# Attention scores: the two components of a head interleaved on TensorE, the causal masks issued ahead of them

## Chip, cores and metric

One core of a Trainium2 chip (trn2) runs the whole program in one launch. The metric is device microseconds (us) of one execution, the median of several; lower is better.

## What is computed

One inference step of a two-layer decoder: a prompt of 1024 tokens and eight sample tokens go through RMSNorm, a joint input projection, a pooling mixer beside differential attention (4 heads), an output projection and a convolution-gated FFN. The change lies in the prompt's attention:

```
def diff_core(q, k, v, q_pos, k_pos, lam):
    s = jnp.einsum('bqhcd,bkhcd->bhcqk', q, k).astype(F32) * (HEAD_DIM ** -0.5)
    mask = k_pos[None, :] <= q_pos[:, None]
    s = jnp.where(mask, s, -jnp.inf)
    p = jax.nn.softmax(s, axis=-1)
    a = p[:, :, 0] - lam * p[:, :, 1]
    return jnp.einsum('bhqk,bkhe->bqhe', a.astype(v.dtype), v)
```

Each head has two components `c` of 64 dimensions, with a softmax each; their difference weighs the values. HEAD_DIM is 64, VDIM is 128, and queries are taken in 8 blocks of 128.

## The kernel before

All 1032 tokens stay in SBUF with the features on the partitions. A head runs in two parts. First come its projections (`up_unit`, L921), pooling and key reshaping, and the pooling half of the output projection (`down_part`, L950). Then comes the attention of its 8 query blocks, in the order `ORDER = [7, 0, 6, 1, 5, 2, 4, 3]`: step s handles block i = ORDER[s], whose scores are (i+1)*128 wide. Two layers of four heads make eight such attentions.

`qT` and `kT` hold component 0 of the head on partitions 0 to 63 and component 1 on partitions 64 to 127. PSUM has two groups of three banks (`group0`, `group1`, guarded by the semaphores `g_free` and `g_full`), one bank for transposes (`t_bank`), one for outputs (`o_bank`); the third bank of each group holds the transposes of the attention weights (`p_bank`) and the sample outputs (`s_bank`). Component 0 of a step takes one group, component 1 the other.

One step s crosses the engines like this:

- TensorE, `scores(s)`: for each component, after a wait for its group, the score matmuls against the keys before the block (L1085, at most 512 columns each), the block on the diagonal (L1088), and the mask, a bf16 product that adds minus 2^100 above the diagonal (L1090), with the semaphore increment that says that the group is full.
- VectorE, `maxima(s)`: for each component the row maximum (L1460) and from it the bias (L1461).
- ScalarE, `exps(s)`: for each component the exponential with its row sum (L764), which frees the group.
- VectorE, `combine(s)`: joins the two components (L1470, L1471, L1474).
- TensorE, `weigh(s)`: transposes of the weights (L1112), for steps 4 to 7 the sample values (`values`, L1097), then the product with the values (L1132), once ScalarE has copied the transposes (L792, L796). `turn_out(s - 1)` (L1141) follows.

TensorE's queue is written out by hand: `scores(0)`, the value transposes `turn("v", ...)` (L1056), and then for each s: `scores(s + 1)`, `weigh(s)`, `turn_out(s - 1)`, with the sample softmax after step 1 (L1166, L1168) and its weights after step 3 (L1157). ScalarE's queue for step s is `mix(s - 2)` (L780), `squares(s - 1)` (L774), the copies of the transposes, `exps(s + 1)`; VectorE's is `mix(s - 2)` (L1489), `combine(s)`, `normalise(s - 1)` (L1483), `maxima(s + 1)`. Ahead of `exps(0)` ScalarE copies the transposed values (L751), issues the store of them (L754) and splits a weight tile (L630).

Of the kernel before, what the change touches and what calls it, by code (L numbers as in the profile page):

```python
# [17 lines left out]
P = 128  # L18
# [7 lines left out]
N_HEADS, HEAD_DIM = 4, 64  # L26
# [134 lines left out]
def hybrid_decoder_kernel(nc, x_prompt, x_sample, cache_k, cache_v, state_pool, state_conv, page_table, norm1_g, w_in,  # L161
# [4 lines left out]
    with ExitStack() as ctx:  # L166
        def sb(name, shape, dt=F32):
            return ctx.enter_context(nc.sbuf_tensor(name, shape, dt))

        def sem(name):  # L170
            return ctx.enter_context(nc.semaphore(name))
# [10 lines left out]
        mask = sb("mask", [P, 2, P], BF16)  # L182
# [5 lines left out]
        qT = sb("qT", [P, T])  # L188
        kT = sb("kT", [P, T])
# [20 lines left out]
        bank = ctx.enter_context(nc.psum_tensor("bank", [P, 8, 512], F32))  # L210
# [16 lines left out]
        g_full, g_free = [sem("group0_full"), sem("group1_full")], [sem("group0_free"), sem("group1_free")]  # L227
# [76 lines left out]
        def x_buf(t):  # L304

            if t < 3:
                return scratch[:, 1024 * t:1024 * t + 1024]
            if t < 7:
                return page[:, t - 3, :, :].rearrange("p t d -> p (t d)")
            return (qT, kT)[t - 7][:, 0:1024]  # L310
# [5 lines left out]
        def grp(p):  # L316
            return bank[:, 3 * p:3 * p + 3, :]
# [40 lines left out]
        def use(half, j):  # L358
            return j % 2, half + j // 2

        def use_head(l, h, name):
            return use(G_SETUP // 2 + l * (G_LAYER // 2) + h * (G_HEAD // 2), HG[name])
# [538 lines left out]
        def _(pe):  # L901
            def wait_free(u):
                pe.wait_ge(g_free[u[0]], u[1] + 1)
# [69 lines left out]
            for t in range(QT_N + 1):  # L973
                u = use(0, t)
                wait_free(u)
                pe.wait_ge(x_in[t], 16)
                rows = P if t < QT_N else 8
                g = bank[:, 3 * u[0]:3 * u[0] + 2, :].rearrange("p a b -> p (a b)")
                for k in range(KC):
                    ins = pe.transpose(g[:, k * P:k * P + rows], x_buf(t)[0:rows, k * P:(k + 1) * P],  # L980
                                       ident[0:rows, 0:rows])
                ins.then_inc(g_full[u[0]], 1)
            u = use(0, QT_N + 1)
            wait_free(u)
            pe.wait_ge(params_in, 16 * len(PAR) * DEPTH)
            for l in range(DEPTH):
                ins = pe.transpose(bank[:, 3 * u[0], l * P:l * P + PAR_W], k_tok[0:PAR_W, l, :],
                                   ident[0:PAR_W, 0:PAR_W])
# [27 lines left out]
            with pe.Fori(0, DEPTH) as l:  # L1016
                norm(l * 2, l * T_LAYER)
                with pe.Fori(0, N_HEADS) as h:
                    it = l * N_HEADS + h
                    n0 = l * U_LAYER + h * U_HEAD  # L1020
                    ug = lambda name: use_head(l, h, name)
# [14 lines left out]
                    for n in range(2):  # L1036
                        u = ug(("qb", n))
# [4 lines left out]
                    u = ug(("y",))  # L1042
# [3 lines left out]
                    for t in range(NT):  # L1046
                        ins = pe.matmul(grp(u[0])[:, t, 0:TW], pw[:, :], pool_dd[:, t * TW:(t + 1) * TW],
                                        start=True, stop=True)
# [25 lines left out]

                    def scores(s):
                        i = ORDER[s]
                        width = (i + 1) * P
                        for c in range(2):
                            u = ug(("s", s, c))
                            wait_free(u)  # L1080
                            rows = slice(c * HEAD_DIM, (c + 1) * HEAD_DIM)

                            for n, at in enumerate(range(0, i * P, 512)):
                                w = min(512, i * P - at)
                                pe.matmul(bank[:, 3 * u[0] + n, 0:w], qT[rows, i * P:(i + 1) * P],  # L1085
                                          kT[rows, at:at + w], start=True, stop=True)
                            last = bank[:, 3 * u[0] + i // 4, (i % 4) * P:(i % 4 + 1) * P]
                            pe.matmul(last, qT[rows, i * P:(i + 1) * P], kT[rows, i * P:(i + 1) * P],  # L1088
                                      start=True, stop=False)
                            ins = pe.matmul(last, mask[:, 0, :], mask[:, 1, :], start=False, stop=True)  # L1090
                            ins.then_inc(g_full[u[0]], 1)

                    def values(b):

# [41 lines left out]
                    def turn_out(s):  # L1136
# [5 lines left out]
                                  stop=True).then_inc(t_full, 1)  # L1142

                    scores(0)
                    turn("v", 0, v_T)
                    turn("v", 1, v_T)
                    for s in range(QT_N):
                        if s + 1 < QT_N:
                            scores(s + 1)
                        weigh(s)  # L1150
                        if s >= 1:
                            turn_out(s - 1)
                        if s == WEIGHTS_STEP:

                            pe.wait_ge(soft_sel, it + 1)
                            for j in range(N_PAGES):
                                ins = pe.matmul(s_bank[:, j * 8:j * 8 + 8], soft[:, j * P:(j + 1) * P], sel8,  # L1157
                                                start=True, stop=True)
                            ins.then_inc(weights_full, 1)
                        if s == SOFTMAX_STEP:  # L1160

                            u = ug(("soft",))
                            wait_free(u)
                            pe.wait_ge(k_red, (it + 1) * DEC_BATCH)
                            for j in range(N_PAGES):
                                pe.transpose(bank[0:16, 3 * u[0] + j // 4, (j % 4) * P:(j % 4 + 1) * P],  # L1166
                                             s_score[:, :, :, j], ident)
                            pe.matmul(bank[0:16, 3 * u[0] + 2, 0:1], comp8, ones[:, 0:1], start=True, stop=True  # L1168
                                      ).then_inc(g_full[u[0]], 1)
# [48 lines left out]
            for t in range(QT_N + 1):  # L1218
                rows = P if t < QT_N else 8
                ins = pe.matmul(t_bank[0:rows, t:t + 1], rot[:, t * P:t * P + rows], ones[:, 0:1], start=True,  # L1220
                                stop=True)
            ins.then_inc(t_full, 1)
            pe.wait_ge(y_done, 2 * DEPTH * NT * KC + KC)
            for t in range(QT_N + 1):
                u = use(G_SETUP // 2 + DEPTH * (G_LAYER // 2), t)
                wait_free(u)
                rows = P if t < QT_N else 8
                g = bank[:, 3 * u[0]:3 * u[0] + 2, :].rearrange("p a b -> p (a b)")
                for k in range(KC):
                    ins = pe.transpose(g[0:rows, k * P:(k + 1) * P], resid[:, k, t * P:t * P + rows], ident)  # L1230
# [391 lines left out]
```

## Time and profile before

| | |
|---|---|
| median of 3 runs | 3089.33 us (3088.89 to 3091.76) |
| span of the profiled execution | 3088.1 us |
| TensorE busy | 2837.5 us, 92% of the span |
| VectorE, ScalarE, GpSimd busy | 1545.4, 785.2, 932.2 us |
| mean granted TensorE clock | 0.936 |

The span runs from the first to the last instruction of the profiled execution. The profile gives no other time of that execution: what lies outside its span is seen only against the runs, whose median is 1.2 us above it. A matmul record is modelled at its end, so records of one stream overlap; the start of one record to the start of the next tells the rate. An fp32 matmul shows as two records here (two passes), each with its own weight load (PEld). A weight load starts when the stream ahead of it does, so its start also marks that of the stream before.

### The profile page before, as it was taken

Reading aid. Unit: us, or ns where it says so; the run is one execution under the profiler, and the core shown is the slowest. Engines: PE = TensorE matmul, PEld = TensorE weight load, DVE = VectorE, ACT = ScalarE, POOL = GpSimd, SP = SyncE. Lnnn points to the kernel's source line nnn. Section 1 sums busy time; section 2 is a strip of 40 time slices with the busy share of each in tenths; the row PEclk is TensorE's granted clock in tenths of the full one; section 3 lists DMA queues with packets and bytes.
Section 4 is the critical chain, followed back from the end, with each engine's and each line's share of the span. In section 5 each row is a group of like instructions: output and inputs, shape, how many; then the busy total and the mean of one; then the engine's idle time right before and its main releaser. Section 6 shows DMA issues by size and latency. Waiting matters only on the chain.

```text
span 3088.1 us, 45465 instructions
## 1 busy us (share of the span) xinstructions
PE 2837.5 (92%) x16776; PEld 2587.2 (84%) x16776; DVE 1545.4 (50%) x1931; ACT 785.2 (25%) x1516; POOL 932.2 (30%) x768
## 2 busy tenths in 40 slices
PE   5889898988999999999988989888999999999996
PEld 4768686867999999999876867777789999999996
DVE  5746464555443444444575463647454444443435
ACT  3221313134222222222233131222332222222222
POOL 4624333244212212221254252525242121212220
PEclk7999898988999999999988998889889999999998
DMA  3422222121111111111113222321111111111111
GB/s 119 125 69 66 89 69 82 49 82 38 46 41 41 55 48 41 41 41 47 52 51 98 68 91 68 99 62 58 52 49 41 41 41 51 52 41 41 41 41 55
DMA packets 70800, 184.00 MB, mean 60 GB/s; under 512 B 8014, under 2 KB 28936, under 8 KB 70552
## 3 DMA queue, kind: packets, MB, share of 16 engines
q1 hardware_dynamic: 33352, 105.95, 10.1%
q0 software_dynamic: 18496, 67.58, 7.0%
q10 hardware_dynamic: 18848, 8.96, 1.0%
q8 instruction: 81, 1.33, 0.2%
q14 instruction: 23, 0.19, 0.0%
HBM read 169.27 MB, written 13.64 MB: 59 GB/s over the span
## 4 chain that ended last, share of the span: by engine, by line
PE 51%; issue 29%; POOL 10%; DVE 6%; ACT 2%; SPq 1%; POOLq 0%; ACTq 0%; DMA 0%; DVEq 0%
PE bank L921 22%; PE bank L950 9%; PE bank L1097 4%; POOL w_lo L498 4%; PE bank L1085 4%; PE bank L967 3%; PE bank L939 3%; PE bank L1132 3%; POOL act_lo L525 2%; PE bank L1112 1%; POOL page L562 1%; DVE rot L1412 1%; ACT scratch L764 1%; DVE scratch L1474 1%; POOL page L584 1%
## 5 line engine op out<-in xcount | busy, mean ns | idle before, releaser
L498 POOL TENSOR_TENSOR w_lo<-w_raw,w_hi 128x1024 fp32r<-128x1024 f32 x180 | 441.5, 2454 | 1474.2 <-ACT w_hi L630 1474.0
L1375 DVE TENSOR_TENSOR resid<-bank,resid 128x1032 f32<-128x1032 f32 x400 | 489.9, 1231 | 431.0 <-PE bank L950 431.0
L921 PE MATMUL bank<-act_hi,w_hi 128*128 128x344 f32 x2640 | 570.3, 324 | 0.0
L921 PE MATMUL bank<-act_hi,w_lo 128*128 128x344 f32 x2640 | 560.5, 320 | 0.0
L921 PE MATMUL bank<-act_lo,w_hi 128*128 128x344 f32 x2640 | 556.5, 319 | 0.0
L921 PEld LDWEIGHTS bank<-act_hi,w_hi 128*128 128x128 f32 x2640 | 439.6, 188 | 9.3 <-issue 0.4
L921 PEld LDWEIGHTS bank<-act_hi,w_lo 128*128 128x128 f32 x2640 | 446.3, 189 | 0.0
L921 PEld LDWEIGHTS bank<-act_lo,w_hi 128*128 128x128 f32 x2640 | 439.6, 188 | 0.0
L950 PE MATMUL bank<-mix_hi,w_hi 128*128 128x344 f32 x1200 | 291.5, 352 | 36.3 <-DVE resid L1375 36.3
L950 PE MATMUL bank<-mix_lo,w_hi 128*128 128x344 f32 x1200 | 259.3, 325 | 0.0
L950 PE MATMUL bank<-mix_hi,w_lo 128*128 128x344 f32 x1200 | 258.1, 324 | 0.0
L950 PEld LDWEIGHTS bank<-mix_hi,w_hi 128*128 128x128 f32 x1200 | 188.0, 192 | 73.6 <-DVE resid L1375 42.8
L1543 DVE TENSOR_TENSOR rot<-bank,rot 128x1032 f32<-128x1032 f32 x44 | 54.2, 1233 | 332.0 <-PE bank L921 332.0
L630 ACT ACTIVATE w_hi<-w_raw 128x1024 fp32r<-128x1024 f32 x180 | 188.5, 1048 | 106.5 <-PE bank L967 83.5
L950 PEld LDWEIGHTS bank<-mix_lo,w_hi 128*128 128x128 f32 x1200 | 205.5, 191 | 0.0
L950 PEld LDWEIGHTS bank<-mix_hi,w_lo 128*128 128x128 f32 x1200 | 204.9, 191 | 0.0
L843 ACT ACTIVATE rot<-scratch 128x1024 f32<-128x1024 f32 x44 | 46.7, 1062 | 518.2 <-DVE scratch L1537 518.2
L562 POOL TENSOR_TENSOR page<-page,bq 128x1024 f32<-128x1024 f32 x64 | 156.6, 2465 | 68.0 <-ACT bq L719 67.6
L1085 PE MATMUL bank<-kT,qT 64*128 64x512 f32 (+3 forms) x320 | 133.1, 521 | 7.5 <-DVE resid L1375 4.7
L1097 PE MATMUL bank<-page,rot 128*8 128x128 f32 x1024 | 130.7, 291 | 0.0
L1369 DVE TENSOR_TENSOR resid<-bank,resid 128x688 f32<-128x688 f32 x120 | 104.9, 875 | 40.3 <-PE bank L967 36.1
L1097 PEld LDWEIGHTS bank<-page,rot 128*8 128x8 f32 x1024 | 95.6, 96 | 32.6 <-issue 6.7
(235 smaller groups left out, 3661.9 us busy)
## 6 DMA issues: line engine op xcount, KB each, us to landing
w_raw<-in_w_up SPq DMA_DIRECT2D x88, 512.0 KB, 3.5
w_raw<-in_w_down SPq DMA_DIRECT2D x44, 512.0 KB, 3.4
w_raw<-in_w_in SPq DMA_DIRECT2D x32, 512.0 KB, 3.4
w_raw<-in_w_out SPq DMA_DIRECT2D x16, 512.0 KB, 3.4
out<-v_tok ACTq DMA_DIRECT2D x16, 512.0 KB, 3.4
page<-in_x_prompt SPq DMA_DIRECT2D x4, 512.0 KB, 9.6
out<-page SPq DMA_DIRECT2D x4, 512.0 KB
out<-rows_out ACTq DMA_DIRECT2D x104, 4.0 KB
```

The source lines that it names most:

```text
L498: pool.tensor_tensor(w_lo[:, slot, :], w_raw[:, slot, :], w_hi[:, slot, :].bitcast(F32), ALU.subtract).then_inc(w_lo_done, 1)
L562: pool.tensor_tensor(kp, kp, q_row, ALU.mult).then_inc(k_mul, 1)
L630: act.activation(w_hi[:, off % SLOTS, :], w_raw[:, off % SLOTS, :], ACT.Copy).then_inc(w_hi_done, 1)
L921: ins = pe.matmul(g[:, t, 0:TW], w[:, slot, k * P:(k + 1) * P], x[:, k, t * TW:(t + 1) * TW], start=(k == 0 and n_ == 0), stop=(k == KC - ...
L939: ins = pe.matmul(g[:, T_ORDER[i], 0:TW], w[:, slot, k * P:(k + 1) * P], x[:, k, tile_of(i)], start=(k == 0 and n_ == 0), stop=(k == KC - ...
L950: ins = pe.matmul(g[:, t, 0:TW], w[:, slot, m * P:(m + 1) * P], x[:, t * TW:(t + 1) * TW], start=(n_ == 0), stop=(n_ == 2))
L967: ins = pe.matmul(grp(u[0])[:, a, 0:TW], w[:, slot, m * P:(m + 1) * P], x[:, tile_of(i)], start=(n_ == 0), stop=(n_ == 2))
L1085: pe.matmul(bank[:, 3 * u[0] + n, 0:w], qT[rows, i * P:(i + 1) * P], kT[rows, at:at + w], start=True, stop=True)
L1097: ins = pe.matmul(s_bank[0:8, 0:P], spread[:, t, b, :], page[:, b % 4, t, :], start=(b == 0 and t == 0), stop=False)
L1132: ins = pe.matmul(o_bank[:, 0:P], a_T[:, r, n * P:(n + 1) * P], v_tok[:, b, :], start=(b == 0), stop=(b == i))
L1369: dve.tensor_tensor(rows, grp3(u[0])[:, 0:2, :], rows, ALU.add).then_inc(g_free[u[0]], 1)
L1375: dve.tensor_tensor(tiles(resid[:, m, :]), grp3(u[0]), tiles(resid[:, m, :]), ALU.add).then_inc(g_free[u[0]], 1)
```

## The change

Only `scores` changes. For both components it first waits for the group and issues the mask, now the product that starts the accumulation in the bank that holds the diagonal. Then the score matmuls follow, component 0 and component 1 in turn for each piece of the keys, then the two diagonal blocks, each with its group's increment. The products and their shapes are the same.

```
                     def scores(s):
                         i = ORDER[s]
-                        width = (i + 1) * P
-                        for c in range(2):
-                            u = ug(("s", s, c))
+                        both = (ug(("s", s, 0)), ug(("s", s, 1)))
+                        halves = (slice(0, HEAD_DIM), slice(HEAD_DIM, 2 * HEAD_DIM))
+                        for u in both:
                             wait_free(u)
-                            rows = slice(c * HEAD_DIM, (c + 1) * HEAD_DIM)
-
-                            for n, at in enumerate(range(0, i * P, 512)):
-                                w = min(512, i * P - at)
+                            pe.matmul(bank[:, 3 * u[0] + i // 4, (i % 4) * P:(i % 4 + 1) * P], mask[:, 0, :],
+                                      mask[:, 1, :], start=True, stop=False)
+
+                        for n, at in enumerate(range(0, i * P, 512)):
+                            w = min(512, i * P - at)
+                            own = n < i // 4
+                            for u, rows in zip(both, halves):
                                 pe.matmul(bank[:, 3 * u[0] + n, 0:w], qT[rows, i * P:(i + 1) * P],
-                                          kT[rows, at:at + w], start=True, stop=True)
-                            last = bank[:, 3 * u[0] + i // 4, (i % 4) * P:(i % 4 + 1) * P]
-                            pe.matmul(last, qT[rows, i * P:(i + 1) * P], kT[rows, i * P:(i + 1) * P],
-                                      start=True, stop=False)
-                            ins = pe.matmul(last, mask[:, 0, :], mask[:, 1, :], start=False, stop=True)
-                            ins.then_inc(g_full[u[0]], 1)
+                                          kT[rows, at:at + w], start=own, stop=own)
+                        for u, rows in zip(both, halves):
+                            pe.matmul(bank[:, 3 * u[0] + i // 4, (i % 4) * P:(i % 4 + 1) * P],
+                                      qT[rows, i * P:(i + 1) * P], kT[rows, i * P:(i + 1) * P],
+                                      start=False, stop=True).then_inc(g_full[u[0]], 1)
```

TensorE's order at step 0 (block 7), from the first score matmul to the value transposes. `bank` is PSUM; the last figures are the shape of the output. Before:

```order
L1085 MATMUL bank<-kT,qT 128x512 [waits group1_free]
L1085 MATMUL bank<-kT,qT 128x384
L1088 MATMUL bank<-kT,qT 128x128
L1090 MATMUL bank<-mask 128x128
L903 REGISTER_ALU
L1085 MATMUL bank<-kT,qT 128x512 [waits group0_free]
L1085 MATMUL bank<-kT,qT 128x384
L1088 MATMUL bank<-kT,qT 128x128
L1090 MATMUL bank<-mask 128x128
L906 REGISTER_ALU
L1056 MATMUL bank<-con,rot 128x128 [waits tbank_free]
```

and now:

```order
L1081 MATMUL bank<-mask 128x128 [waits group1_free]
L903 REGISTER_ALU
L1081 MATMUL bank<-mask 128x128 [waits group0_free]
L1088 MATMUL bank<-kT,qT 128x512 x2
L1088 MATMUL bank<-kT,qT 128x384 x2
L1091 MATMUL bank<-kT,qT 128x128 x2
L906 REGISTER_ALU
L1056 MATMUL bank<-con,rot 128x128 [waits tbank_free]
```

Both masks and both waits moved to the front, and each x2 is one matmul of either component.

TensorE's order at step 2 (block 6), which stands behind `weigh(0)` and ahead of the transposes of step 1. Before:

```order
L1085 MATMUL bank<-kT,qT 128x512 [waits group1_free]
L1085 MATMUL bank<-kT,qT 128x256
L1088 MATMUL bank<-kT,qT 128x128
L1090 MATMUL bank<-mask 128x128
L903 REGISTER_ALU
L1085 MATMUL bank<-kT,qT 128x512 [waits group0_free]
L1085 MATMUL bank<-kT,qT 128x256
L1088 MATMUL bank<-kT,qT 128x128
L1090 MATMUL bank<-mask 128x128
L1104 REGISTER_ALU
L1112 MATMUL bank<-con,scratch 128x128 [waits pbank_free,att_weights]
```

and now:

```order
L1081 MATMUL bank<-mask 128x128 [waits group1_free]
L903 REGISTER_ALU
L1081 MATMUL bank<-mask 128x128 [waits group0_free]
L1088 MATMUL bank<-kT,qT 128x512 x2
L1088 MATMUL bank<-kT,qT 128x256 x2
L1091 MATMUL bank<-kT,qT 128x128 x2
L1106 REGISTER_ALU
L1114 MATMUL bank<-con,scratch 128x128 [waits pbank_free,att_weights]
```

The first component's last product, which lets VectorE begin, stood fourth of eight and now stands seventh of eight.

## Rows read from the trace of the kernel before

**Rows 1.** The page: the chain that ended last, by engine and line.
```profile
PE bank L921 22%; PE bank L950 9%; PE bank L1097 4%; POOL w_lo L498 4%; PE bank L1085 4%; PE bank L967 3%; PE bank L939 3%; PE bank L1132 3%; POOL act_lo L525 2%; PE bank L1112 1%; POOL page L562 1%; DVE rot L1412 1%; ACT scratch L764 1%; DVE scratch L1474 1%; POOL page L584 1%
```

**Rows 2.** First head's attention: us, busy of PE, PEld, DVE, ACT, POOL, then PEclk.
```profile
136.70:213.60 76.90, 64.10 (x379) 47.12 (x379) 34.88 (x92) 27.56 (x77) 23.01 (x41) 0.89 0.24 76
```

**Rows 3.** Waits of TensorE, whole span: waiter <- awaited: us, times, longest.
```profile
PE bank L1112 <- DVE scratch L1474: 32.6, 26, 2.0
```

**Rows 4.** Timeline of the weight loads, step 0, component 0: start us, us.
```profile
137.32 0.19 PEld L1085 LDWEIGHTS bank<-kT,qT 64*128 64x128 f32 x1 [0.24 <-issue]
137.75 0.19 PEld L1085 LDWEIGHTS bank<-kT,qT 64*128 64x128 f32 x1 [0.24 <-issue]
138.07 0.51 PEld L1088 LDWEIGHTS bank<-kT,qT 64*128 64x128 f32 x2
138.70 0.10 PEld L1090 LDWEIGHTS bank<-mask 128*128 128x128 bf16 x1
138.86 0.29 PEld L1085 LDWEIGHTS bank<-kT,qT 64*128 64x128 f32 x2
```

**Rows 5.** Timeline, step 0, from its scores to its exponentials.
```profile
136.78 1.77 PE L1085 MATMUL bank<-kT,qT 64*128 64x512 f32 x4 [0.57 <-DVE resid L1375]
...
140.85 0.61 PE L1056 MATMUL bank<-con,rot 128*128 128x128 f32 x4
...
143.53 0.40 ACTq L754 DMA_DIRECT2D out<-v_tok  x1
144.05 1.06 ACT L630 ACTIVATE w_hi<-w_raw 128x1024 fp32r<-128x1024 f32 x1 [0.56 <-ACT v_tok L751]
145.01 1.10 ACT L764 ACTIVATE scratch<-bank,stat 128x1024 f32<-128x1024 f32 x1
```

**Rows 6.** Timeline, scores of step 2 and what follows them.
```profile
153.54 1.55 PE L1085 MATMUL bank<-kT,qT 64*128 64x512 f32 x4
...
155.51 1.09 DVE L1460 TENSOR_REDUCE stat<-bank 128x1 f32<-128x896 f32 x1
...
157.11 0.23 PE L1090 MATMUL bank<-mask 128*128 128x128 bf16 x1
157.18 0.28 PE L1112 MATMUL bank<-con,scratch 128*128 128x128 f32 x1
...
157.67 1.00 ACT L764 ACTIVATE scratch<-bank,stat 128x896 f32<-128x896 f32 x1
...
160.10 1.01 ACT L805 ACTIVATE bq<-bank 16x1024 f32<-16x1024 f32 x1 [0.31 <-PE bank L1168]
```

**Rows 7.** Timeline, step 4: the first maximum, and TensorE's next wait.
```profile
169.15 0.95 DVE L1460 TENSOR_REDUCE stat<-bank 128x1 f32<-128x768 f32 x1
...
172.30 3.26 PE L1157 MATMUL bank<-small,bq 16*128 16x8 f32 x16 [0.46 <-DVE small L1515]
```

**Rows 8.** Timeline, scores of step 5, in head 0 and in head 1.
```profile
175.49 1.22 PE L1085 MATMUL bank<-kT,qT 64*128 64x256 f32 x2
...
176.91 1.02 DVE L1474 SCALAR_TENSOR_TENSOR scratch<-scratch,stat 128x768 f32<-128x768 f32 x1
...
178.95 1.49 PE L1112 MATMUL bank<-con,scratch 128*128 128x128 f32 x6
...
341.61 0.70 PE L1085 MATMUL bank<-kT,qT 64*128 64x256 f32 x2
...
344.10 1.11 PE L1112 MATMUL bank<-con,scratch 128*128 128x128 f32 x4 [0.28 <-DVE scratch L1474]
```

**Rows 9.** Timeline, steps 6 and 7: the weights joined, then transposed.
```profile
188.36 0.62 DVE L1474 SCALAR_TENSOR_TENSOR scratch<-scratch,stat 128x384 f32<-128x384 f32 x1 [0.23 <-DVE stat L1471]
...
189.72 0.50 PE L1112 MATMUL bank<-con,scratch 128*128 128x128 f32 x3
...
196.04 0.88 DVE L1474 SCALAR_TENSOR_TENSOR scratch<-scratch,stat 128x640 f32<-128x640 f32 x1
...
197.18 0.72 PE L1112 MATMUL bank<-con,scratch 128*128 128x128 f32 x5
```

## The prediction

> **What bounds the kernel now.** I read the page's chain first. Most of it is the projections, which the change doesn't touch; the score matmuls L1085 hold 4% [rows 1], some 120 us. They lie in the eight attentions, so I took the first head's apart. It lasts 76.90 us, with TensorE busy for 64.10, at a mean granted clock of 0.89 [rows 2]. The reader is to see that TensorE isn't saturated there: it waits for others, others for it, and a shorter score block is worth only what the next wait leaves of it. Over all eight heads the transposes L1112 waited 26 times for `combine` (L1474), 32.6 us in all [rows 3]: in every head at steps 0, 2 and 7, which makes 24, and twice at step 4. (The scores of step s stand ahead of the transposes of step s - 1.) In the other steps TensorE came to the transposes last, its scores just ahead of them. There the change can pay.
>
> **The price of a score block.** The passes of 512 columns follow each other by 137.75 - 137.32 = 0.43 us, those of 384 by 138.07 - 137.75 = 0.32 [rows 4]. By columns, 256 take 0.21 and 128 take 0.107. Each fp32 product is two passes. From the start of a block (136.78) to the first even pass are 0.43 + 0.11, so the first weight load costs 0.11 [rows 4, 5]. The diagonal's passes begin at 138.39 and last 0.21; the mask's load starts at 138.70, so going from 64 rows of the array to 128 costs 0.10. From the mask back to 64 rows takes 0.16 [rows 4], against 0.07 from a mask to another product of 128 rows [rows 6]. With S for the passes of one product of each width (block 7: 0.43 + 0.32 + 0.107), a block takes 4S + 0.65 now: 3.42 + 0.65 = 4.07, which is what stands between 136.78 and 140.85 [rows 5].
>
> Afterwards both masks come first (0.07, then 0.16), one weight load is bare (0.11), and one change back remains (0.10): 0.44 of fixed cost in place of 0.65. **This 0.21 is sure**, if the halves cost nothing to alternate.
>
> The rest hangs on what the trace of before never shows: a product on rows 0 to 63 directly followed by one on rows 64 to 127. Bound it from both sides. At worst each change of half costs what a change between 64 and 128 rows does, 0.10 to 0.16 [rows 4]. At best the two halves stream side by side. I take the best, since a score product fills 64 rows and leaves the others empty, and the two components share neither array rows, nor input partitions, nor banks. Starts stay in program order, and a pass must wait for the one before it on its own half. So the second component starts one pass late, and a block takes w + 2S + 0.44, w being its first pass. The gain of a block is then 2S - w + 0.21: 1.49 for block 7 (1.71 - 0.43 + 0.21), 1.28 for block 6, 1.06 for 5, 0.85 for 4, 0.74 for 3, 0.64 for 2, and 0.21 for 1 and 0. A block of 128 columns gains less still, one weight load per 0.11 being all that shows.
>
> The Trainium skill ("TensorE: Matmul & The Clock Gate", Part 3) says that matmuls whose operands lie on different row groups run at the same time, and gives 3.07 times for four groups of 32 rows. No row of before can confirm it, and the figure is for another split. "TensorEngine Tiling (Array Packing)", Key Properties, says that changing the tiling mode drains the engine while changing the tile doesn't; the 0.10 and 0.16 agree with the first half. By a drain at every change of tile the result would be the third case below.
>
> **What each step's scores keep of it.**
> - Step 0 (block 7). The value transposes at 140.85 follow the scores; ScalarE copies them, issues the store at 143.53, splits a weight tile at 144.05 and begins the exponentials at 145.01 [rows 5]. All of it hangs in a row behind TensorE, and the maxima are done long before. 1.49 is kept.
> - Step 1 (block 0) runs while ScalarE and `combine(0)` work, and the same at step 3: 0. Here the change adds a wait, since component 0 now waits for component 1's group as well. Behind it stand only the transposes, which wait for `combine` anyway.
> - Step 2 (block 6). Scores start at 153.54, transposes at 157.18, and at 157.67 come the exponentials [rows 6]. Now the block ends at 153.54 + 0.44 + 1.93 = 155.91. Component 0 is full some 0.2 earlier, at about 155.75, later than before: its maximum started at 155.51. With 1.09 for the maximum and 0.2 for the bias its exponentials start at 157.1, not 157.67. 0.5 is kept, and passes on to the sample softmax, whose copy waits for TensorE (160.10).
> - Step 4 (block 5). VectorE begins the maximum at 169.15, when it is free, and everything up to L1157 (172.30) hangs on VectorE [rows 7]. 0, though TensorE gains 1.06.
> - Step 5 (block 2). In head 0 the passes run at 1.2 GHz (1.22 us for the two where head 1 takes 0.70). The transposes start at 178.95, while L1474 is done at 177.93, so 0.95 of some 1.1 is kept. In head 1, at 2.4 GHz, they wait for VectorE anyway [rows 8]. Two of the 26 waits are of this kind [rows 3], so six heads are like head 0: 6 x 0.95 / 8 = 0.7 a head.
> - Step 6 (block 4): transposes at 189.72, L1474 done at 188.98. 0.67 of 0.85. Step 7 (block 3): 197.18 against 196.92, so 0.18 of 0.74 [rows 9].
>
> The sum is 1.49 + 0.5 + 0.7 + 0.67 + 0.18 = 3.5 us a head, 28 us in eight heads. TensorE saves 1.49 + 0.21 + 1.28 + 0.21 + 1.06 + 0.7 + 0.85 + 0.74 = 6.5 us a head, and 3.0 of it ends as waiting. No DMA, no instruction of another engine is added or dropped; the weight loads for the next head are issued far ahead. Against the span of 3088.1 this gives 3060; the median of the runs is 1.2 us above the span, so I forecast **3061 us**.
>
> **The rivals.**
> 1. *Alternating, but one after the other.* The product count is the same, and nothing in the trace shows an overlap. Blocks gain only 0.21, and component 0 is full late: at step 2 at 156.8 instead of before 155.51, which moves both exponentials back by 0.5. At step 4 it is full at about 169.6, against 169.15, and this hits VectorE's chain: 0.45. Steps 0, 5, 6 and 7 give 0.21, 0.2, 0.21 and 0.18. Net 0.8 - 0.95 = -0.15 a head: 3089.3 + 1 = 3090.5.
> 2. *Slower: every change of half drains.* A block with p products for each component then has 2p - 1 such changes, at 0.10 us each: 5 in blocks 7, 6 and 5, 3 in 4, 3 and 2. At steps 0, 2 and 4 this adds 0.5 each, at 5, 6 and 7 about 0.3 each. Net -0.15 - 1.5 - 0.9 = -2.55 a head, 3089.3 + 20 = 3110. It decides as soon as a change costs over 0.02 us. For it speaks only that the change between 64 and 128 rows has such a price.
> 3. *Overlap, but the clock takes part of it.* The mean clock is 0.89 in the attention [rows 2] and TensorE would be idle for 3 us more in each head. If one further stretch of the 3 us kind runs at 1.2 GHz in each head, it costs up to 1.5 us a head: 28 - 12 = 16, so 3073. Step 5 shows that such stretches occur here [rows 8].
>
> **How the numbers follow.** Overlap as summed has a chance of 0.55, overlap with a loss to the clock or with only part of the streams side by side 0.16, one after the other 0.18, drains 0.11. The predicted time is the likeliest, 3061. Its own range is 3052 to 3069: down if heads run at 1.2 GHz where a kept block stands (each such block doubles its gain), up if step 5 keeps nothing (5.6 us). For 8 in 10 the range takes in the clock's case and one after the other: 3052 to 3092; it leaves out the drains and strays below. A measurement of this kernel can tell about 0.2%, 6.2 us, from no change. Faster by more than that: the overlap cases less a little, 0.70. Within: one after the other nearly whole and a small overlap, 0.18. Slower: drains, 0.12.
>
> **What would show it.** In the changed profile, the passes of component 1 should start while those of component 0 still stream: the third pass of 512 columns should begin with the second, and the next product 0.86 us after the first pass, not 1.72. From the first mask of step 0 to L1056 there should be 2.6 us, not 4.07, and from the second mask to the next weights 0.16. The first exponential of step 0 should come 1.5 us earlier, step 4's L1157 as late after its maxima as before, and L1112 should wait for L1474 behind the scores of steps 5, 6 and 7 in every head. Passes at 0.43 x 4 with late maxima would mean rival 1, gaps of 0.1 between the halves rival 2. The forecast is wrong if the eight attentions shorten by less than 2 or over 5 us each.

## The result, and the profile after

The changed kernel takes 3060.85 us (median of 4 runs, 3059.01 to 3062.71), against 3090.55 us (4 runs, 3088.89 to 3094.43) of the kernel before: a ratio of 0.9902, 95% interval 0.9888 to 0.9916. The forecast was 3061. The profiled executions have spans of 3088.1 and 3057.2 us, 30.9 apart.

The page after, busy time of each engine, and the chain by line:

```profile
span 3057.2 us, 45465 instructions
...
PE 2763.6 (90%) x16776; PEld 2545.1 (83%) x16776; DVE 1543.2 (50%) x1931; ACT 790.3 (26%) x1516; POOL 932.6 (31%) x768
...
PE bank L921 22%; PE bank L950 8%; PE bank L1099 4%; POOL w_lo L498 4%; PE bank L1134 3%; PE bank L967 3%; PE bank L939 3%; POOL act_lo L525 2%; POOL page L562 2%; PE bank L1114 2%; DVE scratch L1476 2%; DVE rot L1414 1%; POOL page L584 1%; PE bank L1088 1%; DVE stat L1462 1%
```

The score products, 4% of the chain before [rows 1], are down to 1% (L1088); VectorE's combination (L1476) has gone from 1% to 2% in their place. TensorE's busy time fell from 2837.5 to 2763.6 us, by 73.9, while the span fell by 30.9. The instruction count is the same.

The first head's attention after: window, us, busy of PE, PEld, DVE, ACT and POOL, then the granted clock (PEclk). It answers to [rows 2]:

```profile
135.60:210.60 75.00, 56.69 (x378) 43.47 (x378) 34.61 (x91) 28.27 (x77) 22.95 (x41) 0.84 0.25 78
```

TensorE is busy for 7.4 us less in a stretch only 1.9 us shorter, and the clock is down from 0.89 to 0.84. This head is one of the two with the highest clock before. Over all eight attentions TensorE's busy time went from 65.8 to 56.9 us a head and the mean granted clock from 0.865 to 0.842.

**One block.** Timeline after, step 0 of the first head, which answers to [rows 4, 5]:

```profile
135.64 0.23 PE L1081 MATMUL bank<-mask 128*128 128x128 bf16 x1 [0.50 <-DVE resid L1377]
136.78 0.23 PE L1081 MATMUL bank<-mask 128*128 128x128 bf16 x1 [0.91 <-DVE resid L1377]
136.94 0.30 PEld L1088 LDWEIGHTS bank<-kT,qT 64*128 64x128 f32 x4
136.94 1.77 PE L1088 MATMUL bank<-kT,qT 64*128 64x512 f32 x8
137.47 0.19 PEld L1088 LDWEIGHTS bank<-kT,qT 64*128 64x128 f32 x2 [0.24 <-issue]
137.90 0.19 PEld L1088 LDWEIGHTS bank<-kT,qT 64*128 64x128 f32 x2 [0.23 <-issue]
138.22 0.52 PEld L1091 LDWEIGHTS bank<-kT,qT 64*128 64x128 f32 x4
138.55 0.39 PE L1091 MATMUL bank<-kT,qT 64*128 64x128 f32 x4
138.86 0.66 PE L1056 MATMUL bank<-con,rot 128*128 128x128 f32 x4
```

Eight passes take the 1.77 us that four took. The weight loads come in twos at the same instant (137.47, 137.90, a 512 pass of 0.43 apart). So the halves run side by side with no stagger of a pass (the records of a pair start 7 ns apart), in weight loads too. From the second mask to L1056 are 2.08 us, where I had 2.58 from the first mask and so 2.51 from the second. But the second mask stands 1.14 us behind the first: it waits for the group that VectorE still adds to the residual (L1377). Before the change this wait stood behind component 0.

**Steps 2 and 5 to 7**, timeline after, answering to [rows 6, 8, 9]:

```profile
152.64 0.42 PE L1081 MATMUL bank<-mask 128*128 128x128 bf16 x2
...
154.71 0.33 PE L1114 MATMUL bank<-con,scratch 128*128 128x128 f32 x1
154.80 1.09 DVE L1462 TENSOR_REDUCE stat<-bank 128x1 f32<-128x896 f32 x1
...
156.12 1.01 ACT L764 ACTIVATE scratch<-bank,stat 128x896 f32<-128x896 f32 x1 [0.77 <-DVE stat L1463]
...
177.26 1.54 PE L1114 MATMUL bank<-con,scratch 128*128 128x128 f32 x6 [0.51 <-DVE scratch L1476]
...
186.91 0.55 PE L1114 MATMUL bank<-con,scratch 128*128 128x128 f32 x3 [0.63 <-DVE scratch L1476]
...
194.23 0.77 PE L1114 MATMUL bank<-con,scratch 128*128 128x128 f32 x5 [0.91 <-DVE scratch L1476]
```

Block 6 went from 3.64 to 2.07 us (152.64 to 154.71). In step 2 the exponentials now wait for the maximum, where before they waited for ScalarE's copy. Behind the scores of steps 5, 6 and 7 the transposes wait for `combine`, as forecast. TensorE's waits over the whole span, against 32.6 us in 26 times before [rows 3]:

```profile
PE bank L1114 <- DVE scratch L1476: 44.2, 48, 2.0
```

**The clock.** Windows with the same columns as above. Before, the value products of step 0 (from 151.1) and of step 2 (from 164.8):

```profile
151.10:153.60 2.50, 2.50 (x18) 2.38 (x17) 0.81 (x4) 1.30 (x5) 0.00 (x0) 0.78 0.86 320
164.80:166.50 1.70, 1.70 (x15) 1.70 (x16) 1.19 (x2) 1.59 (x6) 0.00 (x0) 1.00 0.00 0
```

and the same products after:

```profile
149.10:152.70 3.60, 3.60 (x18) 3.54 (x18) 0.81 (x4) 1.30 (x5) 0.00 (x0) 0.50 0.59 236
163.70:166.90 3.20, 3.18 (x16) 3.20 (x17) 0.75 (x2) 2.43 (x7) 0.00 (x0) 0.54 0.00 0
```

Now both run at 1.2 GHz nearly throughout (0.50 and 0.54), for 1.1 and 1.5 us more. Averaged over the eight heads the growth is smaller, since most heads had lost part of this before: 3.26 to 3.61 us at step 0 and 2.60 to 3.16 at step 2. Ahead of them TensorE stood idle for longer: 6.6 us a head from the first scores to the value products of step 0, against 5.0, and 3.7 us from the scores to the value products of step 2, against 2.6.

In another place the clock gave time back. Step 7, from the transposes of the weights to the first value product, with the sample's value products between them; the second head before, then after:

```profile
369.50:375.70 6.20, 6.19 (x39) 4.12 (x39) 0.33 (x2) 0.60 (x1) 0.00 (x0) 0.72 0.00 0
365.60:370.20 4.60, 4.56 (x39) 3.38 (x39) 0.37 (x2) 0.60 (x1) 0.00 (x0) 1.00 0.00 0
```

Three of the eight heads took 6.15 us for it before and five took 4.49; now all take 4.49, 0.6 us a head less on average.

### The profile page after: what moved, and what is told of

Its sections match the earlier page's. It is cut to its first block, busy times and chain, and to the rows that moved or that the text cites. A ratio compares the mean times of both kernels' runs of the same rounds, so it can differ in the third digit from the quotient of the medians.

```text
span 3057.2 us, 45465 instructions
## 1 busy us (share of the span) xinstructions
PE 2763.6 (90%) x16776; PEld 2545.1 (83%) x16776; DVE 1543.2 (50%) x1931; ACT 790.3 (26%) x1516; POOL 932.6 (31%) x768
## 4 chain that ended last, share of the span: by engine, by line
PE 48%; issue 30%; POOL 10%; DVE 8%; ACT 2%; POOLq 0%; ACTq 0%; DMA 0%; DVEq 0%; SPq 0%
PE bank L921 22%; PE bank L950 8%; PE bank L1099 4%; POOL w_lo L498 4%; PE bank L1134 3%; PE bank L967 3%; PE bank L939 3%; POOL act_lo L525 2%; POOL page L562 2%; PE bank L1114 2%; DVE scratch L1476 2%; DVE rot L1414 1%; POOL page L584 1%; PE bank L1088 1%; DVE stat L1462 1%
## 5 line engine op out<-in xcount | busy, mean ns | idle before, releaser
L1377 DVE TENSOR_TENSOR resid<-bank,resid 128x1032 f32<-128x1032 f32 x400 | 490.0, 1231 | 428.1 <-PE bank L950 428.1
L950 PE MATMUL bank<-mix_hi,w_hi 128*128 128x344 f32 x1200 | 290.4, 351 | 34.7 <-DVE resid L1377 34.7
L950 PE MATMUL bank<-mix_lo,w_hi 128*128 128x344 f32 x1200 | 260.4, 326 | 0.0
L950 PE MATMUL bank<-mix_hi,w_lo 128*128 128x344 f32 x1200 | 256.9, 323 | 0.0
L950 PEld LDWEIGHTS bank<-mix_hi,w_hi 128*128 128x128 f32 x1200 | 186.6, 191 | 71.9 <-DVE resid L1377 41.4
L950 PEld LDWEIGHTS bank<-mix_lo,w_hi 128*128 128x128 f32 x1200 | 206.1, 192 | 0.0
L950 PEld LDWEIGHTS bank<-mix_hi,w_lo 128*128 128x128 f32 x1200 | 204.4, 191 | 0.0
L1099 PE MATMUL bank<-page,rot 128*8 128x128 f32 x1024 | 124.5, 283 | 0.0
L1099 PEld LDWEIGHTS bank<-page,rot 128*8 128x8 f32 x1024 | 92.7, 93 | 29.3 <-issue 6.7
L1134 PE MATMUL bank<-v_tok,a_T 128*128 128x128 f32 x576 | 103.9, 341 | 9.3 <-ACT a_T L792 8.2
```

The source lines that it names most:

```text
L950: ins = pe.matmul(g[:, t, 0:TW], w[:, slot, m * P:(m + 1) * P], x[:, t * TW:(t + 1) * TW], start=(n_ == 0), stop=(n_ == 2))
L1099: ins = pe.matmul(s_bank[0:8, 0:P], spread[:, t, b, :], page[:, b % 4, t, :], start=(b == 0 and t == 0), stop=False)
L1134: ins = pe.matmul(o_bank[:, 0:P], a_T[:, r, n * P:(n + 1) * P], v_tok[:, b, :], start=(b == 0), stop=(b == i))
L1377: dve.tensor_tensor(tiles(resid[:, m, :]), grp3(u[0]), tiles(resid[:, m, :]), ALU.add).then_inc(g_free[u[0]], 1)
```

## The experiments

All times are medians of up to 12 runs with the kernel before on the same chip (3091.0 to 3093.6 us, and 3090.6 for the change's own). The ratios are to that. They were not all run on one chip, and an interval reaches 3 to 6 us to either side, so a difference of two medians of less than some 6 us shows nothing. Where the text gives "us a head", it is from the last L950 to the first L967 in the profiled execution, averaged over the eight heads.

| kernel | us | ratio, 95% interval |
|---|---|---|
| the change | 3060.85 | 0.9902 (0.9888 to 0.9916) |
| e1_in_turn | 3061.74 | 0.9918 (0.9905 to 0.9932) |
| e2_masks_last | 3061.84 | 0.9909 (0.9894 to 0.9925) |
| e3_values_first | 3059.21 | 0.9902 (0.9886 to 0.9917) |
| e4_fill | 3035.93 | 0.9822 (0.9809 to 0.9836) |
| e5_mask_between | 3092.74 | 1.0002 (0.9993 to 1.0011) |
| e6_before_fill | 3074.75 | 0.9939 (0.9925 to 0.9953) |
| e7_first_more_fill | 3012.90 | 0.9745 (0.9729 to 0.9760) |
| e8_more_fill | 3019.79 | 0.9759 (0.9745 to 0.9772) |
| e9_in_turn_fill | 3059.51 | 0.9894 (0.9876 to 0.9912) |
| e10_fill_waits | 3003.49 | 0.9709 (0.9694 to 0.9725) |

**e1: both masks first, the components in turn.**

```
-                            for u, rows in zip(both, halves):
-                                pe.matmul(... kT[rows, at:at + w], start=own, stop=own)
-                        for u, rows in zip(both, halves):
-                            pe.matmul(... kT[rows, i * P:(i + 1) * P], start=False, stop=True)
+                        for u, rows in zip(both, halves):
+                            for n, at in enumerate(range(0, i * P, 512)):
+                                pe.matmul(... kT[rows, at:at + w], start=own, stop=own)
+                            pe.matmul(... kT[rows, i * P:(i + 1) * P], start=False, stop=True)
```

> Both waits and both masks first, as in the change, but then all products of component 0 and after them all of component 1. Theory A (the gain is the two halves of the array streaming side by side, which needs them to alternate): the blocks take 4S + 0.44 us again; step 0 comes out some 0.9 us later than before the change, since its first product now waits for both groups, and the other kept steps gain about 0.2 each, so 3088 to 3096 us. Theory B (the gain is the masks put together, with fewer changes between 64 and 128 rows, and the alternating does nothing): 3061 to 3070. In the trace, by A, the two components' 512-column passes stand one after another, 0.43 apart.

The time fits theory B and the trace fits neither. Timeline of e1, step 0 of the first head (L1088 the score products, L1090 the diagonal):

```profile
138.53 0.23 PE L1081 MATMUL bank<-mask 128*128 128x128 bf16 x1 [0.91 <-DVE resid L1376]
138.69 2.09 PE L1088 MATMUL bank<-kT,qT 64*128 64x512 f32 x6
140.30 0.38 PE L1090 MATMUL bank<-kT,qT 64*128 64x128 f32 x2
140.62 0.81 PE L1088 MATMUL bank<-kT,qT 64*128 64x384 f32 x2
...
141.58 0.66 PE L1056 MATMUL bank<-con,rot 128*128 128x128 f32 x4
```

Six passes of L1088 begin before the first diagonal. Component 0 has four, so two are component 1's 512-column passes, which stand behind component 0's diagonal in the queue. A product on the free half starts ahead of its turn, and the halves overlap in part without alternating: the block takes 141.58 - 138.53 = 3.05 us, between 3.86 (worked out for one after the other) and 2.08.

Where each component has only two products (blocks 4, 3 and 2, at steps 6, 7 and 5), the scores take as long in turn as alternating, from the first mask to the end of the last product: 1.56, 1.35 and 1.98 us against 1.56, 1.34 and 1.98. So the order matters in the blocks of three products alone. These leave e1 1.5 us behind the change at the transposes of step 1, and it is level at those of step 4 (42.8 us behind the last L950 against 42.7): its mean clock in the attention is 0.865, the change's 0.842.

**e2: alternating, masks last.** `scores` waits for both groups, issues the products in turns and closes with the two masks.

```
-                            wait_free(u)
-                            pe.matmul(... mask[:, 0, :], mask[:, 1, :], start=True, stop=False)
+                            wait_free(u)
...
+                        for u in both:
+                            pe.matmul(... mask[:, 0, :], mask[:, 1, :], start=False, stop=True).then_inc(g_full[u[0]], 1)
```

> Components alternate as in the change, both waits first, but both masks come last again and close the accumulation. Theory A: a block has 0.35 us of fixed cost (0.11 + 0.10 + 2 x 0.07) in place of 0.44, so the time is that of the change within 2 us, 3059 to 3063. Theory B: the gain is gone, 3080 to 3090.

Measured 3061.84, inside A's range. The masks' place at the front is worth nothing that these runs can tell; that no mask stands between the halves is what counts, which the next shows.

**e5: each component behind its own wait and mask, in turn.**

```
+                        for c in range(2):
+                            wait_free(u)
+                            pe.matmul(last, mask[:, 0, :], mask[:, 1, :], start=True, stop=False)
...
+                            pe.matmul(last, qT[rows, i * P:(i + 1) * P], kT[rows, i * P:(i + 1) * P],
+                                      start=False, stop=True).then_inc(g_full[u[0]], 1)
```

> Each component in turn with its own wait and its mask first: wait, mask 0, products 0, wait, mask 1, products 1. The mask of component 1 (128 rows) stands between the halves, so they can't stream side by side as they still did in part in e1_in_turn. Theory A (side by side is what gives the time): blocks as before the change, 4.07 us for block 7, and the time of before within 4 us, 3086 to 3094. Theory B (masks ahead of the products give it, by whatever way): 3062 to 3070.

Measured 3092.74, a ratio of 1.0002: the time of before, and inside A's range. Timeline of e5, step 0 (L1086 the score products, L1088 the diagonal, L1082 the mask):

```profile
135.88 1.77 PE L1086 MATMUL bank<-kT,qT 64*128 64x512 f32 x4
137.49 0.38 PE L1088 MATMUL bank<-kT,qT 64*128 64x128 f32 x2
137.80 0.23 PE L1082 MATMUL bank<-mask 128*128 128x128 bf16 x1
137.96 1.77 PE L1086 MATMUL bank<-kT,qT 64*128 64x512 f32 x4
139.57 0.38 PE L1088 MATMUL bank<-kT,qT 64*128 64x128 f32 x2
```

One product on all 128 rows between the halves, and the second half starts only behind it. The same products with this mask and the wait for the second group moved to the front are e1: 0.84 points less in the ratio, 26 us, and 3.7 us a head (79.69 against 76.01). The wait is no rival at this step, since the mask at 137.80 follows the diagonal without one; in later steps wait and mask were not parted. So the gain is the overlap, and taking the mask out of the middle is the part of the change that brings it.

**e3: the first value transposes ahead of the scores.**

```
-                    scores(0)
                     turn("v", 0, v_T)
+                    scores(0)
                     turn("v", 1, v_T)
```

> The change, with the first four value transposes (turn v 0) ahead of scores(0). In the changed kernel component 0's mask of step 0 is followed by a wait of 0.9 to 1.1 us for the second group (resid L1377), which stood hidden behind component 0 before. Theory C (this wait is on the path and costs most of what the forecast had for step 0): the transposes fill it and the second four start 1.4 us earlier, 8 x 1.4 = 11 us, so about 3050. Theory D (the exponentials of step 0 hang on the maxima or on ScalarE's weight tile, not on this wait): 3059 to 3062.

Measured 3059.21, inside D's range and with the ratio of the change. Yet C's first half is there: averaged over the eight heads, the transposes of the weights of step 0 come 1.6 us earlier after the last L950 than in the change (11.07 against 12.66 us), and those of step 1 come 2.2 earlier. At the end of the attention 0.1 us is left (75.99 against 76.09), since two later stretches now lie at 1.2 GHz more: the sample's value products of step 4 (L1099), from their first to the next L1134, take 5.59 us against 4.51, and step 7 takes 5.90 against 4.49 from its transposes to its value products.

**e4: idle time filled.** The results of the fill are never read.

```
+                    def fill(n, width=512):
+                        for _ in range(n):
+                            pe.matmul(p_bank[:, 0:width], ident, con[:, CON_SMALL:CON_SMALL + width],
+                                      start=True, stop=True)
...
                     turn("v", 1, v_T)
+                    fill(4)
...
+                        if s == SOFTMAX_STEP + 1:
+                            fill(1)
...
                             u = ug(("soft",))
+                            fill(1)
                             wait_free(u)
```

> The change, with idle-filling fp32 products of 512 columns into the free transpose bank, results never read: four after the value transposes, one ahead of the sample softmax's transposes, one ahead of scores(3). Theory E (the shorter score blocks leave TensorE idle and the clock falls to 1.2 GHz behind them, which took back 0.2 us ahead of step 2's scores and 0.8 us in step 2's weights times values): those stretches run at 2.4 GHz, about 1 us a head back, 3053 to 3057, and a mean clock over 0.94. Theory F (the clock falls for another reason, or the fill delays as much as it gives): 3060 to 3068.

Measured 3035.93, far below E's range: work that is thrown away makes the kernel 25 us faster. Timeline and window of e4, first head, value products of step 2 and the attention as a whole:

```profile
163.61 1.80 PE L1134 MATMUL bank<-v_tok,a_T 128*128 128x128 f32 x14 [0.45 <-ACT a_T L792]
...
137.10:210.00 72.90, 58.24 (x393) 41.98 (x394) 34.51 (x91) 28.51 (x78) 23.20 (x41) 0.93 0.26 80
```

The 14 passes take 1.80 us where the changed kernel takes 3.20, and the granted clock is 0.93 in place of 0.84. E's mechanism is shown, its size was 3 times too small: I had counted only what the change lost against before, and the fill also gives back what both kernels lose (e6).

**e6: the kernel before with the same fill** (the diff is that of e4).

> The kernel before with the same six filling products as e4_fill. Theory E (the clock is lost to TensorE's idle time, and the change made more of it): before had the smaller loss, at the value products of step 0 and in steps 2 and 3, about 1.5 us a head, so 3073 to 3080, less than the 25 us that the fill gave after the change; the two filled kernels then differ by 38 to 45 us, more than the 30 us without fill. Theory G (the fill gives the same 25 us to both, and the change's own clock loss is nothing): 3064 to 3068.

Measured 3074.75, inside E's range. Each against the kernel before on its own chip, the fill gives 19 us here (0.9939) and 25 in e4 (0.9822 against the change's 0.9902), which the intervals don't part. The attentions do: 1.5 us a head here (79.08 to 77.59), 3.0 in e4 (76.09 to 73.07). With the fill in both, the change is worth 36 us by the ratios (3074.75 - 3035.93 = 38.8 by medians of two chips) and 4.5 us a head; without, 29.7 and 3.0. So some 6 to 12 us of the change's own gain went to the clock. The fills sit in the same places of the program, not in equal waits, so this is a size and no exact sum.

**e7, e8: more fill, with and without the early value transposes.**

```
+                            fill(1)
+                            fill(1, 256)
                             pe.wait_ge(soft_sel, it + 1)
...
+                        if s == QT_N - 1:
+                            fill(2)
                         weigh(s)
...
+                    fill(1, 256)
                     turn_out(QT_N - 1)
+                    fill(1, 256)
                     turn_out(QT_N)
```

> e3_values_first and e4_fill together, with further fills: one and a half products ahead of the sample weights (L1157), two ahead of weigh(7), half a product ahead of each of the last two turn_out. If the early transposes are worth their 1.4 to 2 us a head once the clock is held, this is 12 to 16 us below e4_fill, and the further fills give up to 1 us a head more: 3012 to 3024. If step 0's gain is eaten by the next wait whatever the clock: 3030 to 3038.

> e4_fill with the further fills of e7_first_more_fill and the value transposes where the change has them. Theory E: the stretches at 1.2 GHz about 36 to 43 us and 74 to 78 us after a head's attention begins go, 3022 to 3032. If they come from the tiny products of L1157 themselves and the waits of the head's end can't be filled without delay: 3034 to 3040.

Measured 3012.90, inside its range, and 3019.79, below its own. The further fills give 16 us (e8 against e4). About half of it lies inside the attentions (72.00 against 73.07 us a head) and half outside: averaged over the heads, the granted clock of the 10 us behind the first L967 went from 0.87 to 1.00. What the early transposes add is not resolved. The medians differ by 6.9 us, but the intervals of the ratios overlap; in the profiled executions (e7's took 3019.57, above its median) the transposes of step 0 come 1.8 us earlier in e7 (11.07 against 12.87), and the attentions end level (72.01 and 72.00), at a mean clock of 0.935 against 0.961. The 11 us expected of them are not reached.

**e9: e1 with the fill of e4.**

> e1_in_turn (both masks first, then component 0, then component 1) with the six filling products of e4_fill. Without fill, in turn and alternating gave the same time within a microsecond. Theory H (alternating does shorten what is on the path, block 7 by 3.05 - 2.08 = 1.0 us and block 6 by some 0.4, and without fill the clock took it back): 8 x 1.4 = 11 us above e4_fill, about 3047. Theory I (once the halves overlap in part, the next wait hides the rest, whatever the clock): 3034 to 3038.

Measured 3059.51, 23.6 us above e4 (22 by the ratios): H's direction, twice its size. Alternating does shorten the path; without fill it seemed worth 1 us. H had block 6 at 0.4 us and block 5 at nothing, but each of the blocks 7, 6 and 5 takes 0.9 to 1.0 us longer in e9 than in e4. Part of the 23.6 us comes from the clock in two heads. In six heads the fill leaves step 1 where e1 has it, its first mask 10.5 us behind the last L950. In the fourth and the eighth the stretch from the scores of step 0 to those of step 1 runs at a granted clock of 0.64, and that mask stands at 15.0. This moves the transposes of step 0 by 3.2 us in both, 6.5 us in all; why the clock fell just there was not tried.

**e10: fill in further waits.**

```
                     for m in range(KC):
+                        for _ in range({2: 1, 4: 3}.get(m, 0)):
+                            pe.matmul(o_bank, ident, con[:, CON_SMALL:CON_SMALL + 512], start=True, stop=True)
                         down_part(1, m, ug(("wg", m)))
...
+                        if s == 0:
+                            fill(1, 384)
```

> e7_first_more_fill with three further fills: three products ahead of part 4 and one ahead of part 2 of the pooling half's output projection (L950), into the free output bank, and one of 384 columns ahead of weigh(0). In e7 the clock still falls some 12 us before each attention, behind TensorE's wait of 2.9 us for VectorE (resid), and in five heads near step 1. If these waits are what lowers it, 1 to 2.5 us a head: 2994 to 3006. If the fill delays L950 or the clock stays low there all the same: 3010 to 3020.

Measured 3003.49, inside the first range and the fastest here, 2.9% below the kernel before (0.9709, 0.9694 to 0.9725). Its mean granted clock is 0.966, against 0.934 of the change:

```profile
core 0: 3001.7 us, clock 0.966
```

## Why the forecast held, and where it didn't

**The total came out of terms that missed both ways, and that they met is in part luck.** The eight attentions, from the last L950 to the first L967, went from 79.08 to 76.09 us on average: 3.0 us each, 24 us, where I had 3.5 and 28. The other 6.9 us of the span's 30.9 lie in parts that the change doesn't touch, 3.7 of them between the sixth head's attention and the seventh's. They are part of one execution's spread and were not traced to a cause.

**The overlap: right in kind, mis-sized.** That the halves stream side by side is shown by e5 against e1 and by the passes in the trace. The step that failed is "Starts stay in program order [...] so the second component starts one pass late". The second component starts with the first, ahead of the first's second pass, and in e1 even ahead of products that are queued before it. Block 7 takes 2.08 us from its second mask (I had 2.51), block 6 takes 2.07 from its first (2.37). TensorE's saving is then larger than my 6.5 us a head; its busy time fell by 73.9 us in all, 9.2 a head. (My 0.21 for block 1 doesn't follow from the formula, which gives 0.53; at step 3 neither is kept.)

**The fixed cost.** My 0.16 from a mask to the 64-row products is there (136.78 to 136.94). That the masks ahead of the products save fixed cost was of no use that shows: e2 takes the same time with the masks last.

**Step 0: 1.49 forecast, 0.59 on average.** This is the largest miss. I asked for the double wait only at steps 1 and 3. At step 0 the second group comes free 1.14 us after the first, because VectorE still adds L950's last part, and component 0 no longer covers this. The faster block made up for some of it, so seven heads gain 0.8. In the sixth the block runs at a granted clock of 0.55 and takes 3.7 us in place of 2.1, and that head loses 0.8. The order of the first transposes gets time back here (e3), but nothing of it was left at the end of the attention.

**Step 2: 0.5 forecast, 0.6 measured** from its scores to the sample softmax's transposes. The new limit is the maximum, as worked out: in the first head the exponentials wait 0.77 us for L1463.

**Step 4: 0 forecast, 0.5 measured** from the end of step 2's value products to the scores of step 5. VectorE set the time of L1157 (L1159 now), as forecast, but L1159 itself starts 0.6 us earlier behind the last L950.

**Step 5: 0.7 forecast, 0.9 measured; step 6: 0.67 and 0.74; step 7: 0.18 and 0.10.** Here `combine` limits all three, and the waits of these transposes for it rose from 26 (L1112) to 48 (L1114).

**The clock was a rival and should have been in the sum, with both signs.** Averaged over the heads, 0.2 us went ahead of step 2's scores, and 0.8 us between the sample softmax and the end of step 2's value products. I had put "one further stretch" a head at 1.5 us, a chance of 0.16. It was smaller than that, since before the change six heads of eight already ran these products partly at 1.2 GHz, and one of them is faster now. And 0.6 us a head came back at step 7, where I had no term for it. With step 0's 0.9 too little and the clock's 1.0 on one side, and this 0.6, step 4's 0.5 and 0.4 more at steps 2, 5 and 6 on the other, the sum came within 0.5 us of the 3.5. Rival 1 fell with e5's contrast, rival 2 with the passes: no gap of 0.1 us stands between the halves.

## What to carry to other kernels

Two products that each use one half of the array's rows and write different banks run at the same time, if nothing on all 128 rows stands between them; look for a mask, a transpose or a bias in the middle before anything else. A shorter TensorE block is worth what the next wait leaves of it, less what the clock takes for the idle time that it makes: read the granted clock of the stretches behind each new wait, in every repeat and not in the first one alone. Where two waits are joined into one, ask at each place which work stood between them.

## What the runs showed of the chip

- Products on rows 0 to 63 and on rows 64 to 127 start in pairs, 7 ns apart, weight loads included: 8 passes in 1.77 us. The Trainium skill ("TensorE: Matmul & The Clock Gate", Part 3) says that matmuls on different row groups overlap; this trace agrees, for fp32 and two halves.
- The same part of the Trainium skill says that matmuls keep the program's order in start and end. In e1 component 1's first product starts ahead of component 0's diagonal (six passes of L1088 before 140.30), so for starts the measurement decides against it.
- With the halves in turn and nothing between them (e1), blocks of two products a component overlap as fully as alternating (1.56 us both for block 4, to the end of its last product), a block of three only in part (3.05 us against 2.08 for block 7).
- A 128-row product (a record of 0.23 us) between the halves stops the overlap: 3.7 us a head, 26 to 31 us over the kernel (e5 against e1).
- Filling TensorE's waits with products that nobody reads gave 25 us (e4), and with more of them and the early transposes 57 us (e10 against the change). The mean granted clock rose from 0.934 to 0.951 and 0.966.
